# One next-key projection chunk spread over the attention groups of a turn, and the lead part's scores spaced by width

## The chip, the cores and the metric

The kernel runs on one core of a Trainium2 chip. The metric is the device time of one launch in microseconds. Three runs of the kernel before took 3239.09, 3241.71 and 3245.02 us; the median, 3241.71 us, is the time to compare with. TensorE (PE) multiplies, VectorE (DVE) and ScalarE (ACT) empty PSUM and do the elementwise work, GpSimd (POOL) splits weights, SyncE (SP) issues the weight loads.

## The reference, cut to what matters

Two blocks run one after the other on 1024 tokens of width 1024. The two parts that the change touches are attentions with 16 heads of width 64:

```
# block 1: forgetting attention ("fox"), causal, 128-token blocks
logits = q k^T * scale + F[t] - F[s];  probs = softmax(masked logits);  o = probs v
y_f = o * silu(g)
# block 2, second mixer ("nb"): 2-D neighbourhood attention with a relative bias,
# 8 rows x 16 columns of keys around each query, plus 256 context tokens
s = q k^T * scale + bias;  p = softmax([s, s_ctx]);  o = p [v, v_ctx];  y = (o * silu(g)) w_out
```

q, k, v and g are projections of the same input (`u @ w_in`). Everything else (the recurrent branch, the windowed mixer, output projections, norms) is outside the change.

## The kernel before, in words

Every float32 product is done as three fast products of high and low parts: w_hi u_hi, w_hi u_lo, w_lo u_hi. A weight unit is 128 output columns (one pair of heads). SP loads units in a fixed order, POOL splits each into w_hi and w_lo (L210, L212) into one of two slots, as soon as PE signals that the unit two places earlier is used up. A projection chunk is 8 tiles x 3 parts = 24 matmuls (FULL) of up to 512 columns into one PSUM bank; its last matmul signals.

Both attentions are instances of one class, Flow, each with 8 turns (one for each pair of heads). A planner (`plan`) writes one list of steps for a turn, and PE, ACT and DVE each walk it in this order, doing their share and waiting on semaphores:

- F n: PE does the next n matmuls of the projection stream (L1304). For fox the stream in a turn is V0 V1 G0 G1 of this turn, then Q0 Q1 K0 K1 of the next (192 matmuls); nb has V0 V1 V2, G0 G1, Q0 Q1, K0 K1 K2 (240; V2 and K2 are the 256 context columns). Chunks of a turn alternate between two PSUM banks, and a chunk's first matmul waits until the chunk two places earlier has been taken out.
- E: a finished chunk is taken out. For a key or query chunk ACT casts the high part (L1578, L1581, L2423, L2426) and DVE subtracts the low part (L1602, L1606, L2470, L2474). Key and query chunks finished before the turn's last score are held until it has been issued.
- S: a piece of scores on PE (L1334), then DVE's masked reduction of it (L1455). The next S on PE waits for that reduction. The first S of a turn also waits for the last key chunk's low part.
- X: ACT's exponential (L1384). T: transposes on PE (L1350; L1345 for v, L1355 for the row sums), cast on ACT (L1393), low part on DVE (L1466). V: probs times v on PE (L1368).
- I, M, O, N: inverse row sums (L1484, L1486), the half swap of the output (L1407), its sum (L1494) and its product with the inverse sums (L1479).
- W, Y, D: silu on ACT (L1411); y times silu on DVE (L1504), then ACT's cast of y (L1416); D is DVE's low part of y (L1509) and ACT's two stores (L1426).
- L, B: ACT's load of the next turn's mask rows, and DVE's preparation of them in two parts (L1614 for fox, two instructions a part in L2450 and L2453 for nb).

A turn has three parts. The lead runs 24 matmuls for each V chunk, with the four score pieces of segment 0 at places 6 to 49 of the stream. The groups (20 in fox, 26 in nb) are one T each, with S, V and fill spread so that after the last group the stream stands at `main`: the end of the Q chunks. The tail runs what is left: K0 and K1 (and K2) stand beside the last events, W, Y, D and B. The last of the eight turns has no Q or K.

In fox, before the change, the steps from the last V on are: V, L, F4 N F4 I F4 M F4 O F4 N, W, Y, F4, E(K0), D, B, F24, E(K1), B, and the next turn begins F6 S F8 S. In nb they are V, L, F4 M F4 O F4 N, W, Y, F12, E(K0), D, B, F24, E(K1), B, F24, E(K2), then F6 S F14 S.

Of the kernel before, what the change touches and what calls it, by code (L numbers as in the profile page):

```python
# [15 lines left out]
P = 128  # L16
# [39 lines left out]
def build_program(nc, a):  # L56
# [3 lines left out]
    def sb(name, shape, dt=F32, at=None):  # L60
        return (at or ctx).enter_context(nc.sbuf_tensor(name, shape, dt))
# [4 lines left out]
    with ctx:  # L66
# [234 lines left out]
        scores = sb("scores", [P, 8, P], at=ph2)  # L301
# [690 lines left out]
        class Flow:  # L992
# [110 lines left out]
            def plan(self, before, turns, final, tables, last_fill, side_by_side=False):  # L1103
# [5 lines left out]
                FULL = 3 * KT  # L1109
# [3 lines left out]
                def chunks_of(units, scores_before, side_by_side=False):  # L1113
                    new = []
                    parts = [(unit, i) for unit in units for i in range(len(unit[3]))]
                    if side_by_side:
                        parts.sort(key=lambda part: part[1] >= 2)
                    for (kind, it, unit, spans), i in parts:
                        c0, n = spans[i]
                        last, seq = i == len(spans) - 1, len(self.chunks)  # L1120
                        beside = side_by_side and seq < 4
                        b = (self.p_bank, self.p_bank + 1, self.o_bank, self.o_bank + 1)[seq] if beside \
                            else self.p_bank + seq % 2
                        count[final[kind]] += 1
                        count["chunk"] += not last
                        ch = {"kind": kind, "it": it, "unit": unit, "c0": c0, "n": n, "first": i == 0,
                              "last": last, "seq": seq, "scored": scores_before, "bank": b, "beside": beside,
                              "waits": self.user.get(b),
                              "done": (w_used, unit + 1) if last else (self.chunk, count["chunk"]),
                              "out": ({"act": self.act_out, "dve": self.dve_out}[final[kind]], count[final[kind]])}  # L1130
                        self.user[b] = ch["out"]
                        self.chunks.append(ch)
                        new.append(ch)
                    return new

                def group(kind, it, **more):
                    g = {"kind": kind, "n": count["G"], "it": it, **more}
                    count["G"] += 1
                    if kind != "N":
                        count["high"] += 1  # L1140
                        g["high"] = count["high"]
                    return g
# [11 lines left out]
                for it, units in enumerate(turns):  # L1154
                    fill = chunks_of(units, count["S"] + n_scores)
                    steps, held = [], []
                    at = {"fill": 0, "S": 0}

                    scores, base_u = [], count["U"]
# [11 lines left out]
                    def fill_to(n):  # L1171
                        n = min(n, FULL * len(fill))
                        while at["fill"] < n:
                            part = min(n - at["fill"], FULL - at["fill"] % FULL)
                            steps.append(("F", part))
                            at["fill"] += part
                            if at["fill"] % FULL == 0:
                                ch = fill[at["fill"] // FULL - 1]
                                if ch["kind"] in "QK" and at["S"] < n_scores:
                                    held.append(ch)  # L1180
                                else:
                                    steps.append(("E", ch))

                    def score(s):
                        s["l_free"] = l_turned[s["seg"] % 2]
                        steps.append(("S", s))
                        at["S"] += 1
                        if at["S"] == n_scores:
                            steps.extend(("E", ch) for ch in held)

                    def exponentials(n):
                        while due and n:
                            steps.append(("X", *due.pop(0)))
                            n -= 1
# [1 line left out]
                    due, final_turn = [], it == len(turns) - 1  # L1196
                    values = [ch for ch in fill if ch["kind"] == "V"]
                    lead = FULL * len(values)
                    places = [(6 + (lead - 14) * i // len(scores[0]), "S", s) for i, s in enumerate(scores[0])]
                    places += [(FULL * (i + 1) + 9, "T", ch) for i, ch in enumerate(values)]  # L1200
                    for pos, what, x in sorted(places, key=lambda place: place[0]):
                        fill_to(pos)
# [7 lines left out]
                    exponentials(4)  # L1210
                    groups = [self.seg_groups(seg) for seg in range(len(self.segments))]
                    n_groups = sum(len(g) for g in groups)
                    start, main = at["fill"], FULL * sum(ch["kind"] in "VGQ" for ch in fill)
                    if final_turn:
                        n_groups = last_fill
                    todo, waiting, done = [], None, 0
# [1 line left out]
                    def event():  # L1218
                        if todo:
                            what, *rest = todo.pop(0)  # L1220
                            steps.append(("T", group("N", it, seg=rest[0], seg_n=rest[1])) if what == "N" else
                                         (what, *rest))

                    for seg, rows in enumerate(groups):
                        count["seg"] += 1
                        pending = list(scores[seg + 1]) if seg + 1 < len(scores) else []
                        for i, (items, adds) in enumerate(rows):
                            g = group("P", it, seg=seg, seg_n=count["seg"], items=items, adds=adds, starts=i == 0,
                                      ends=i == len(rows) - 1, exped=base_u + self.first_unit(seg + 1))
                            steps.append(("T", g))  # L1230
                            l_turned[seg % 2] = g["n"] + 1
                            exponentials(1)
                            share = -(-len(pending) // (len(rows) - i))
                            for s in pending[:share]:
                                score(s)
                                due += [(s, hd) for hd in range(2) if s["end"]]
                            del pending[:share]
                            done += 1
                            goal = start + (main - start) * min(done, n_groups) // n_groups
                            fill_to((at["fill"] + goal) // 2)  # L1240
                            if i == 0:
                                todo.append(("I", seg, g["exped"]))
                            if waiting:
                                steps.append(("V", waiting))
                                if waiting["ends"]:
                                    s0 = (waiting["seg"], waiting["seg_n"])
                                    todo[-1:-1] = [("M", it, *s0), ("O", it, *s0), ("N", *s0)]
                                    if self.early and final_turn and seg == len(groups) - 1:
                                        todo.append(("W", it))
                                        for part, cols in enumerate(self.early):  # L1250
                                            todo += [("D", it, self.early[part - 1])] if part else []
                                            todo.append(("Y", it, cols))
                                event()
                            waiting = g
                            fill_to(goal)
                            if i == len(rows) - 1:
                                exponentials(4)
# [1443 lines left out]
```

## Time and profile before

| | |
|---|---|
| median of three runs | 3241.71 us |
| profiled execution, first to last instruction (span) | 3236.3 us |
| PE busy | 3109.7 us, 96% |
| DVE busy | 1999.7 us, 62% |
| ACT busy | 1299.9 us, 40% |
| POOL busy | 759.8 us, 23% |
| mean granted TensorE clock | 0.988 |

The span is one execution, 5.4 us shorter than the median run. Busy time of PE counts overlapping matmuls once, and their ends are modelled, so starts are what to read. "Idle before" stands in brackets behind a row, with what ended it. Fox's turns run from 601.7 to 1209.2 us, nb's from 2346.2 to 3095.4 us.

### The profile page before, as it was taken

The numbers are of one execution on the slowest core, as the hardware profiler recorded it, in microseconds if no ns is written. First come the engines' busy times: TensorE is split into PE (matmuls) and PEld (weight loads), VectorE is DVE, ScalarE is ACT, GpSimd is POOL, SyncE is SP. The second block draws the span as 40 slices with busy tenths as digits, with TensorE's granted clock in tenths as the row PEclk, the third lists the DMA queues.
The fourth block names the chain that finished last, engine by engine and source line by source line (L and its number), as shares of the span: only waits on it lengthen the run. The fifth ranks groups of instructions, "written<-read, shape, count | busy, mean of one in ns | idle before, by whom it ended". The sixth has DMA issues, their size and how long they took to land.

```text
span 3236.3 us, 47842 instructions
## 1 busy us (share of the span) xinstructions
PE 3109.7 (96%) x18134; PEld 2578.9 (80%) x18134; DVE 1999.7 (62%) x3834; ACT 1299.9 (40%) x2340; POOL 759.8 (23%) x324
## 2 busy tenths in 40 slices
PE   9999999999999989999899999999899999999987
PEld 6888888777777767877799889888677778777765
DVE  5676677555565657975755555556755555655555
ACT  5534443444444440022444444440344444454412
POOL 3223332322222213543211121113112112111221
PEclk9999999999999999999999999999999999999999
DMA  3111111111111137521200010153201111100141
GB/s 118 46 40 46 46 59 46 60 59 53 53 53 53 64 146 298 220 79 52 91 30 30 31 43 30 46 203 130 78 21 51 45 51 45 51 32 33 67 161 76
DMA packets 64828, 237.79 MB, mean 73 GB/s; under 512 B 7008, under 2 KB 10080, under 8 KB 63600
## 3 DMA queue, kind: packets, MB, share of 16 engines
q1 hardware_dynamic: 31680, 115.91, 9.9%
q10 hardware_dynamic: 32944, 119.10, 9.7%
q8 instruction: 135, 2.21, 0.3%
q14 instruction: 69, 0.57, 0.0%
HBM read 185.11 MB, written 49.87 MB: 73 GB/s over the span
## 4 chain that ended last, share of the span: by engine, by line
PE 79%; DVE 9%; ACT 5%; issue 2%; DVEq 2%; DMA 1%; ACTq 1%; SPq 0%
PE ps L1304 21%; PE ps L189 13%; PE ps L360 9%; PE ps L2223 7%; PE ps L1368 5%; PE ps L1334 4%; PE ps L1350 4%; PE ps L891 3%; PE ps L482 3%; PE ps L868 2%; PE ps L133 2%; DVE fox_l L1455 1%; PE ps L852 1%; DVE wa_l L941 1%; PE ps L853 1%
## 5 line engine op out<-in xcount | busy, mean ns | idle before, releaser
L210 POOL TENSOR_TENSOR w_hi<-raw,small 128x1024 fp32r<-128x1024 f32 x160 | 334.9, 2093 | 2393.7 <-PE ps L1304 1099.3
L212 POOL TENSOR_TENSOR w_lo<-raw,w_hi 128x1024 fp32r<-128x1024 f32 x160 | 424.8, 2655 | 22.8
L1304 PE MATMUL ps<-nb_u_hi,w_hi 128*128 128x512 f32 (+1 forms) x640 | 249.2, 389 | 6.1 <-DVE nb_q_lo L2470 4.2
L1304 PE MATMUL ps<-nb_u_hi,w_lo 128*128 128x512 f32 (+1 forms) x640 | 246.6, 385 | 0.0
L1304 PE MATMUL ps<-nb_u_lo,w_hi 128*128 128x512 f32 (+1 forms) x640 | 245.7, 384 | 0.0
L1466 DVE TENSOR_TENSOR nb_pt_lo<-ps,nb_pt_hi 128x512 fp32r<-128x512 f32 x208 | 143.9, 692 | 144.2 <-ACT nb_pt_hi L1393 143.9
L360 PE MATMUL ps<-u_hi,w_hi 128*128 128x512 f32 x528 | 212.8, 403 | 5.9 <-ACT silu_h L539 2.6
L1304 PE MATMUL ps<-u_hi,w_lo 128*128 128x512 f32 x512 | 208.9, 408 | 0.0
L360 PE MATMUL ps<-u_hi,w_lo 128*128 128x512 f32 x528 | 208.6, 395 | 0.0
L360 PE MATMUL ps<-u_lo,w_hi 128*128 128x512 f32 x528 | 208.4, 395 | 0.0
L1304 PE MATMUL ps<-u_hi,w_hi 128*128 128x512 f32 x512 | 208.3, 407 | 0.0
L1304 PE MATMUL ps<-u_lo,w_hi 128*128 128x512 f32 x512 | 207.5, 405 | 0.0
L1393 ACT CAST nb_pt_hi<-ps 128x512 fp32r<-128x512 f32 x208 | 122.1, 587 | 193.4 <-PE ps L1350 190.7
L1466 DVE TENSOR_TENSOR fox_pt_lo<-ps,fox_pt_hi 128x512 fp32r<-128x512 f32 (+1 forms) x160 | 102.0, 638 | 129.3 <-ACT fox_pt_hi L1393 128.8
L2223 PE MATMUL ps<-wa_u_hi,w_hi 128*128 128x512 f32 (+1 forms) x480 | 173.1, 361 | 4.3 <-DVE wa_u_lo L2156 1.9
L891 PE MATMUL ps<-wa_v,wa_pt 128*128 128x64 f32 x1344 | 176.5, 266 | 0.0
L2223 PE MATMUL ps<-wa_u_lo,w_hi 128*128 128x512 f32 (+1 forms) x480 | 171.1, 356 | 0.0
L2223 PE MATMUL ps<-wa_u_hi,w_lo 128*128 128x512 f32 (+1 forms) x480 | 171.0, 356 | 0.0
L902 ACT ACTIVATE wa_l<-wa_l,wa_nm 128x641 f32<-128x641 f32 (+2 forms) x160 | 119.3, 746 | 124.8 <-DVE wa_nm L941 123.6
L891 PEld LDWEIGHTS ps<-wa_v,wa_pt 128*128 128x128 f32 x1344 | 168.9, 192 | 0.0
L1393 ACT CAST fox_pt_hi<-ps 128x512 fp32r<-128x512 f32 (+1 forms) x160 | 87.0, 544 | 144.8 <-PE ps L1350 144.3
L1304 PEld LDWEIGHTS ps<-nb_u_hi,w_hi 128*128 128x128 f32 x640 | 121.6, 190 | 29.3 <-issue 11.6
(357 smaller groups left out, 8027.8 us busy)
## 6 DMA issues: line engine op xcount, KB each, us to landing
raw<-in_w_stream SPq DMA_DIRECT2D x160, 512.0 KB, 3.3
h_sb<-in_w_ada ACTq DMA_DIRECT2D x16, 1024.0 KB, 5.0
nf_b<-nf_rows ACTq DMA_DIRECT2D x16, 512.0 KB, 4.4
nb_bias<-in_rel_bias ACTq DMA_DIRECT2D x16, 448.0 KB, 3.8
y_parts<-wa_y_hi ACTq DMA_DIRECT2D x8, 640.0 KB, 3.0
y_parts<-wa_y_lo ACTq DMA_DIRECT2D x8, 640.0 KB, 4.2
la_out_yh<-y_parts SPq DMA_DIRECT2D x8, 640.0 KB, 10.0
la_out_yl<-y_parts SPq DMA_DIRECT2D x8, 640.0 KB, 11.1
```

The costliest lines, as they stand in the source:

```text
L189: mm = pe.matmul(out, w(slot, tiles[i]), u[:, first + i, cols], start=start and i == 0 and p == 0, stop=stop and i == len(tiles) - 1 and p ...
L210: pool.tensor_tensor(w_hi[:, s, :], raw[:, s, :], zero, ALU.add)
L212: pool.tensor_tensor(w_lo[:, s, :], raw[:, s, :], w_hi[:, s, :].bitcast(F32), ALU.subtract).then_inc(w_ready, 1)
L360: mm = pe.matmul(ps[:, b:b + CH], w(slot, k), u[:, k, ch["c"] * CH:(ch["c"] + 1) * CH], start=k == 0 and p == 0, stop=k == KT - 1 and p == 2)
L891: mm = pe.matmul(ps[:, o0:o0 + HD], self.pt[0:n, self.v_place[g] % 3, (c - c0) * P:(c - c0 + 1) * P], vals[0:n, vb, cols], start=c == 0, s ...
L1304: mm = pe.matmul(ps[:, b:b + ch["n"]], w(slot, k), u[:, k, ch["c0"]:ch["c0"] + ch["n"]], start=k == 0 and p == 0, stop=k == KT - 1 and p == 2)
L1334: mm = pe.matmul(ps[:, o:o + n], q[r, qc], k[r, key:key + n], start=p == 0, stop=p == 2)
L1350: mm = pe.transpose(out[:, j * P:(j + 1) * P], self.l_of(g["seg"], qi, hd)[:, l0:l0 + P], ident)
L1368: mm = pe.matmul(ps[:, o + o0:o + o0 + n], self.v[:, vb, kv if self.shared else hd, :], pt[:, g["high"] % 2, p0:p0 + n], start=g["starts"] ...
L1393: nc.scalar.copy(self.pt_hi[:, g["high"] % 2, 0:w], ps[:, t:t + w]).then_inc(self.high, 1)
L1466: dve.tensor_tensor(self.pt_lo[:, i, 0:w], ps[:, t:t + w], self.pt_hi[:, i, 0:w].bitcast(F32), ALU.subtract).then_inc(self.freed, 1)
L2223: mm = pe.matmul(ps[:, b * CH + t:b * CH + t + n], w(i % 2, k), u[:, k, t:t + n], start=k == 0 and p == 0, stop=k == KT - 1 and p == 2)
```

## The change

Two edits in `plan`; a third line changes no order, since no piece of segment 0 is ever in the list of a later segment.

```diff
-                    places = [(6 + (lead - 14) * i // len(scores[0]), "S", s) for i, s in enumerate(scores[0])]
+                    ahead = scores[0]
+                    sizes = [sum(n for _, _, n in s["blk"]["pieces"][s["piece"]]["runs"]) + 3 * P // 2 for s in ahead]
+                    places = [(6 + (lead - 14) * sum(sizes[:i]) // sum(sizes), "S", s) for i, s in enumerate(ahead)]
...
-                    start, main = at["fill"], FULL * sum(ch["kind"] in "VGQ" for ch in fill)
+                    first_k = [ch for ch in fill if ch["kind"] == "K"][:1]
+                    start, main = at["fill"], FULL * (sum(ch["kind"] in "VGQ" for ch in fill) + len(first_k))
...
-                        pending = list(scores[seg + 1]) if seg + 1 < len(scores) else []
+                        pending = [s for s in scores[seg + 1] if s not in ahead] if seg + 1 < len(scores) else []
```

Score places in the lead (in matmuls of the stream): fox 6, 14, 23, 31 become 6, 17, 22, 33 (widths 512, 128, 512, 256); nb 6, 20, 35, 49 become 6, 23, 35, 52 (widths 512, 256, 512, 256). In seven of eight turns of each flow `main` grows by 24, from 144 to 168 in fox and from 168 to 192 in nb: chunk K0 is now done between the groups, and the tail has one 512-column key chunk less. The tail's steps are now, in fox: V, L, F4 N F4 I F4 M F4 O F4 N, W, Y, F4, E(K1), D, B, B, and the next turn begins F6 S F11 S. In nb: V, L, F4 M F4 O F4 N, W, Y, F12, E(K1), D, B, F24, E(K2), B, then F6 S F17 S. No instruction is added or removed on any engine.

## Rows read from the trace of the kernel before

**Rows 1.** The page, busy time of each engine (us, share, instructions).
```profile
PE 3109.7 (96%) x18134; PEld 2578.9 (80%) x18134; DVE 1999.7 (62%) x3834; ACT 1299.9 (40%) x2340; POOL 759.8 (23%) x324
```

**Rows 2.** Stretch, length, busy PE PEld DVE ACT POOL, clock, DMA: fox, nb groups.
```profile
850.60:897.90 47.30, 46.03 (x293) 36.76 (x292) 29.05 (x88) 23.84 (x55) 6.56 (x4) 1.00 0.07 23
...
2653.40:2714.20 60.80, 58.80 (x408) 47.17 (x406) 38.89 (x94) 31.62 (x61) 7.51 (x4) 1.00 0.05 18
```

**Rows 3.** Waits of PE, fox turn 832.0:909.4 (total us, times, longest).
```profile
PE ps L1334 <- DVE fox_nm L1455: 0.9, 3, 0.4
PE ps L1350 <- DVE fox_pt_lo L1466: 0.6, 1, 0.6
```

**Rows 4.** Waits of PE, nb turn 2632.7:2728.2.
```profile
PE ps L1350 <- ACT nb_l L1384: 1.4, 2, 0.8
PE ps L1334 <- DVE nb_nm L1455: 0.5, 1, 0.5
```

**Rows 5.** Timeline of PE, end of a fox turn (start, duration, ..., idle before).
```profile
903.98 0.39 PE L1304 MATMUL ps<-u_hi,w_hi 128*128 128x512 f32 x1
...
909.47 0.39 PE L1304 MATMUL ps<-u_hi,w_hi 128*128 128x512 f32 x1
...
911.13 0.49 PE L1334 MATMUL ps<-fox_k_hi,fox_q_hi 64*128 64x512 f32 x2
...
914.43 0.33 PE L1334 MATMUL ps<-fox_k_hi,fox_q_hi 64*128 64x128 f32 x2 [0.29 <-DVE fox_nm L1455]
```

**Rows 6.** Timeline of ACT, the same stretch.
```profile
905.10 1.05 ACT L1416 CAST fox_y_hi<-fox_y 128x1024 fp32r<-128x1024 f32 x1 [3.27 <-DVE fox_y L1504]
906.05 0.58 ACT L1581 CAST fox_k_hi<-ps 128x512 fp32r<-128x512 f32 x1
```

**Rows 7.** Timeline of DVE, the same stretch.
```profile
903.84 1.23 DVE L1504 TENSOR_TENSOR fox_y<-fox_y,fox_silu 128x1024 f32<-128x1024 f32 x1
906.66 0.69 DVE L1606 TENSOR_TENSOR fox_k_lo<-ps,fox_k_hi 128x512 fp32r<-128x512 f32 x1 [1.60 <-ACT fox_k_hi L1581]
907.27 1.22 DVE L1509 TENSOR_TENSOR fox_y<-fox_y,fox_y_hi 128x1024 f32<-128x1024 f32 x1
908.40 1.22 DVE L1614 TENSOR_TENSOR nf_tri<-nf_b,consts 128x1024 f32<-128x1024 f32 x1
...
910.90 1.86 DVE L1614 TENSOR_TENSOR nf_tri<-nf_b,consts 128x1024 f32<-128x1024 f32 x1
912.94 0.75 DVE L1455 CUSTOM_DVE_ANT_0 fox_l<-ps,nf_b,fox_top 128x512 f32<-128x512 f32 x1 [0.18 <-issue]
```

**Rows 8.** Timeline of POOL, the same stretch.
```profile
909.78 1.89 POOL L210 TENSOR_TENSOR w_hi<-raw,small 128x1024 fp32r<-128x1024 f32 x1 [7.53 <-PE ps L1304]
911.82 3.19 POOL L212 TENSOR_TENSOR w_lo<-raw,w_hi 128x1024 fp32r<-128x1024 f32 x1
```

**Rows 9.** Timeline, fox's third segment: a transpose group of PE, a low part of DVE.
```profile
889.11 0.60 PE L1350 MATMUL ps<-consts,fox_l 128*128 128x128 f32 x4
...
889.67 0.69 DVE L1602 SCALAR_TENSOR_TENSOR fox_q_lo<-ps,fox_q_hi 128x512 fp32r<-128x512 f32 x1
```

**Rows 10.** Timeline of DVE, end of an nb turn.
```profile
2722.61 2.09 DVE L2450 TENSOR_TENSOR nb_bias<-nb_bias,consts 128x896 f32<-128x896 f32 x2
...
2728.85 0.42 DVE L2474 TENSOR_TENSOR nb_k_lo<-ps,nb_k_hi 128x256 fp32r<-128x256 f32 x1 [0.34 <-ACT nb_k_hi L2426]
```

**Rows 11.** Timeline of PE, the first score of the nb turn that follows.
```profile
2729.71 0.50 PE L1334 MATMUL ps<-nb_k_hi,nb_q_hi 64*128 64x512 f32 x2
```

**Rows 12.** Timeline of POOL beside four back-to-back DVE subtractions (L1850).
```profile
1404.46 2.48 POOL L210 TENSOR_TENSOR w_hi<-raw,small 128x1024 fp32r<-128x1024 f32 x1 [5.68 <-PE ps L189]
```

**Rows 13.** Timeline of DVE, the same stretch.
```profile
1403.97 8.54 DVE L1850 TENSOR_TENSOR r_lo<-h_sb,r_hi 128x1024 fp32r<-128x1024 f32 x4
```

**Rows 14.** A long wait of PE elsewhere in the kernel, and the stretch around it.
```profile
1259.77 0.79 PE L189 MATMUL ps<-y_hi,w_hi 128*128 128x512 f32 x1 [3.34 <-DMA y_lo<-y_parts]
```

**Rows 15.** Busy time by stretch around that wait (columns as in rows 2).
```profile
1259.00:1264.00 5.00, 4.23 (x12) 3.38 (x13) 0.37 (x1) 0.00 (x0) 1.97 (x1) 0.66 1.03 409
```

## The prediction

> **What bounds the kernel now.** I read the page first: PE is busy 96% of the span, the next engine 62% [rows 1]. So PE's order sets the time, and an edit of the order can only change how long PE waits. Then the busy time by stretch: in a fox turn the groups take 47.30 us, of which PE is idle 1.3; in an nb turn 60.80 with 2.0 idle [rows 2]. The waits of PE give the reasons. A fox turn has 0.9 us for the reduction of scores (three waits, one of them the 0.29 in the lead) and 0.6 for a low part [rows 3]; an nb turn 1.4 us for exponentials and 0.5 for a reduction [rows 4]. The tails show no wait at all. All turns are alike, so one stands for seven. What the groups can give back at most is 7 x 1.3 + 7 x 1.9 = 22 us. What the tail hides must be read from ACT, DVE and POOL there.
>
> **Unit of the sum.** A full key chunk takes PE 909.47 - 903.98 = 5.49 us, 0.229 a matmul [rows 5]. PE's work stays the same. The change takes 5.49 us out of each tail and puts it between the groups, so anything in the tail that was less than 5.49 us early becomes late.
>
> **Fox, end of the turn.** DVE multiplies y by silu from 903.84 to 905.07 [rows 7]. ACT casts y from 905.10 and only then takes out the key chunk (906.05 to 906.63) [rows 6]; DVE's low part ends at 907.35 [rows 7]. Before, that chunk is K0, and K1 with its 5.49 us still follows. Now it is K1, and the next turn's first score needs it. PE would like that score at 911.13 - 5.49 = 905.64 and gets it about 0.1 after 907.35: a wait of 1.8 us where there was hardly one. The whole row y, cast, key cast, key low part keeps its place, because it hangs on PE's steps after the last V, which are the same.
>
> The second score waits for DVE's reduction of the first. Between them DVE still has D (1.22) and the two mask preparations (1.22 each, the 1.86 being a delayed one) [rows 7], and none of these now stands beside K1. Free of delay they end at 910.9, the reduction (begun 0.18 later, 1.5 for two heads) at 912.5. PE, with F11 in place of F8, would like the second score at 907.45 + 0.9 + 11 x 0.229 + 0.2 = 911.1. That is a wait of 1.4, where 0.4 was (0.29 shown [rows 5] and the least gap that is not shown): 1.0 more.
>
> Now POOL. It starts a split 0.31 us after the first matmul behind the last key chunk (909.78 against 909.47) [rows 5, 8]. DVE's second mask instruction, begun at 910.90, took 1.86 and ended 1.1 after POOL's 1.89 us instruction: it waited for POOL's end and then ran its 1.22. POOL's next one took 3.19 [rows 8], and had to wait in turn. So a subtraction or addition with both inputs in SBUF and POOL's split exclude each other. The Trainium skill, "SBUF — State Buffer", section "SBUF: two separate sides", says this as a rule: whichever starts first keeps the shared port for its whole instruction and the other fully blocks; the trace agrees, 1.86 against 1.22. With K1 done 5.49 earlier the split begins at 904.29, beside y times silu, waits for its end at 905.07, and its second instruction begins near 907.0, 0.3 us before D (907.27). That one takes about 2.4 (3.19 less its wait of 0.8), so D begins at 909.35, not 907.27, and the second score waits 2.1 more. I take this: 1.0 + 2.1 + 0.1 for the drains = 3.2 for the second score. The other end is 1.0.
>
> **Fox, groups.** Half-groups go from F2 to F3. Two waits on reductions and some gaps too short to be shown lose one matmul, 0.23 each: about -0.7. The pt_lo wait of 0.55 in the third segment is different: Q1 now ends there too. Q0 is held until the last score and its low part ends at 889.67 + 0.69 = 890.36 [rows 9]. K0 uses the same bank, and its first matmul comes right behind Q1, where PE now has transposes (889.11) [rows 9]: it waits 1.3 us. This swallows the 0.55. Net of the groups: -0.7 - 0.6 + 1.3, with the small gaps -0.2 at most; bounds -1.3 (all waits gone, none new) and +0.3. Fox a turn: 1.8 + 3.2 - 0.2 = 4.8; seven turns 34 us.
>
> **nb, end of the turn.** One more chunk (K2, 24 short matmuls) stands behind K1, so K1's cast is no problem. The first score would like to start at 2729.71 - 5.49 = 2724.2 [rows 11]. DVE's two mask additions run 2722.61 to 2724.70 and K2's low part (0.42) is queued behind them [rows 10]: the score starts at 2725.2, a wait of 1.0. That is the lower end. POOL's split now arrives at 2723.1, in the first of the two. In the other place where POOL arrived during back-to-back SBUF subtractions, it went in after the first: four of 1.22 took 8.54 us [rows 13], and POOL's took 2.48 [rows 12]. Then the second addition is 1.9 late, and the wait is 2.9, with 0.2 behind it: 3.1. I take 2.7, nearer to the row. **nb, groups:** the extra matmul stands in each stretch in which a wait ended, and the two waits for exponentials (0.7 each) lose two matmuls or the cast of a gate chunk ahead of them: -0.4 each, the reduction -0.2, small gaps -0.4: -1.4 (bounds 0 and -1.9 shown, -2.5 with the small gaps). nb a turn: 2.7 - 1.4 = 1.3; seven turns 9 us.
>
> **The spacing by width** moves fox's second score by 3 matmuls, which is counted above; alone it would save the 0.3 of [rows 5]. In nb's leads and in turn 0 nothing waits, so it costs nothing; its cover is the 2 us and more between each reduction's end and the next score. DMAs: the same loads and stores from the same queue; y's stores go out 2 us later in fox, and the next turn needs y's buffer only in its second segment. The mask rows are asked for at the last V and needed about 10 us later.
>
> **Clock.** After a wait of 3.34 us [rows 14] PE ran at a mean of 0.66 over 5 us [rows 15], 1.2 GHz for 3.4 us, against 2.4 before: 5 x 0.34 = 1.7 us lost. The fox junction now has a wait of about 3.3 us, two and a half us after one of 1.8. I count the fall in half of the seven turns: 6 us. Bounds: none, and all 14 junctions, 24.
>
> **Sum.** 34 + 9 + 6 = 49 us on the profiled execution: span 3236.3 to 3285. That execution is 5.4 below the median; the same 49 on 3241.7 gives **3291 us**, 1.5% slower.
>
> **Rivals.**
> (a) POOL and DVE miss each other: the order of arrivals shifts by 0.3 us and D goes first. For: 0.3 us is little. Against: the rows repeat to 0.02 us, and a POOL instruction then only waits and blocks the mask additions. Fox 1.8 + 1.0 - 0.2 = 2.6, nb 1.0 - 1.4 = -0.4: 18 - 3, so 3257.
> (b) The clock falls at every junction. For: nb's wait is near 3 us. Against: nb's wait is shorter than the 3.34 of that row. 43 + 24: 3309.
> (c) Faster: the tail's chain y, cast, key cast runs early enough, and only the groups' gain is left. It decides at one point: whether DVE starts y times silu at least 1.8 us sooner than 903.84 when counted from the last V. For: the other split, of the V unit, started at the turn's last V before and now comes earlier, so DVE's steps of the tail have POOL beside them less. Against: y hangs on PE's last pair of transposes, which keeps its place. Fox -1.3, nb -1.4 to -1.9: -20, so 3222.
> (d) No measurable change: the new waits are as long as the old ones, both flows near 0; 3242. It needs (a) and half of (c).
>
> **From cases to numbers.** My forecast 0.62, (a) 0.17, (b) 0.09, (c) 0.06, (d) 0.06. The forecast's own range, by the bounds of nb (1.0 to 3.1), of fox's groups (-1.3 to +0.3) and the clock (0 to 12), is 3270 to 3302. For 8 in 10 I add (a) and most of (b): **3254 to 3308**. About 0.2%, 6.5 us, is what can be told from no change here: faster 0.06, the same 0.06, slower 0.88.
>
> **What would show it.** In the profile after: at each fox junction a wait of PE for k_lo of about 2 us, then one for the reduction (nm) of about 3.3; D in fox taking about 3.3 us instead of 1.22 and a POOL instruction of 2.6 just before; a wait of 1.3 at a projection matmul in fox's third segment for q_lo; nb's first score waiting 1 to 3 us for the low part of K2; nb's waits for exponentials down from 1.4 to about 0.6 a turn. I am wrong if the first score of a fox turn starts within 0.5 us of when PE reaches it, or if fox turns (77 us before, the stretch of [rows 3]) are shorter than 78.

## The result: 1.9% slower, and the profile after

The changed kernel takes 3303.82 us (median of 5 runs, 3298.78 to 3313.21) beside 3244.45 us before (5 runs); the ratio is 1.0189 [1.0173, 1.0204]. The forecast was 3291 us, a change of +49; measured are +59 between the medians and +67 between the two profiled spans. Its profiled execution took 3305.42 us. The measured time lies just above the forecast's own range (3270 to 3302) and inside the wider one (3254 to 3308). In the kernel after, the lines of Flow stand 3 lower: L1337 is L1334 of before. "First score" of a turn is its first S, "second score" the next one.

| | before | after |
|---|---|---|
| span of the profiled execution | 3236.3 us | 3303.6 us |
| mean granted TensorE clock | 0.988 | 0.978 |
| first score to first score, fox turns | 77.0 us | 81.8 to 84.4 us (the first one 78.4) |
| first score to first score, nb turns | 95.5 us | 96.8 to 99.8 us |

The busy line of the page answers to [rows 1]. PE is busy 26 us more for the same 18134 instructions. The work is the same and the mean granted clock is lower, so more of it ran at the lower clock.

```profile
PE 3136.0 (95%) x18134; PEld 2599.5 (79%) x18134; DVE 2017.2 (61%) x3834; ACT 1304.3 (39%) x2340; POOL 765.7 (23%) x324
```

The waits of PE over the whole program (total us, times, longest): the first three did not exist at this size before. Each stands at the seven junctions between turns (the second has the short waits of [rows 3] in it too). The fourth, once in each of seven fox turns, is the new wait for the shared PSUM bank.

```profile
PE ps L1337 <- DVE nb_k_lo L2477: 18.5, 7, 2.6
PE ps L1337 <- DVE fox_nm L1458: 18.2, 16, 3.3
PE ps L1337 <- DVE fox_k_lo L1609: 13.8, 7, 2.0
PE ps L1307 <- DVE fox_q_lo L1605: 8.5, 7, 1.2
```

The end of a fox turn, PE first. It answers to [rows 5]: the first score waits 1.97 us; its first pair of matmuls takes 0.70 us where it took 0.49, because the clock falls to half just then. The second starts 7.00 us after the first, where it was 3.30.

```profile
931.08 0.70 PE L1337 MATMUL ps<-fox_k_hi,fox_q_hi 64*128 64x512 f32 x2 [1.97 <-DVE fox_k_lo L1609]
...
938.08 0.33 PE L1337 MATMUL ps<-fox_k_hi,fox_q_hi 64*128 64x128 f32 x2 [1.78 <-DVE fox_nm L1458]
```

DVE in the same place, against [rows 7]: the chain y times silu, low part of the key, D, two mask preparations, reduction is the same, but D takes 3.12 us and not 1.22.

```profile
927.42 1.22 DVE L1507 TENSOR_TENSOR fox_y<-fox_y,fox_silu 128x1024 f32<-128x1024 f32 x1
930.24 0.69 DVE L1609 TENSOR_TENSOR fox_k_lo<-ps,fox_k_hi 128x512 fp32r<-128x512 f32 x1 [1.60 <-ACT fox_k_hi L1584]
930.85 3.12 DVE L1512 TENSOR_TENSOR fox_y<-fox_y,fox_y_hi 128x1024 f32<-128x1024 f32 x1
933.90 2.51 DVE L1617 TENSOR_TENSOR nf_tri<-nf_b,consts 128x1024 f32<-128x1024 f32 x2
936.59 0.75 DVE L1458 CUSTOM_DVE_ANT_0 fox_l<-ps,nf_b,fox_top 128x512 f32<-128x512 f32 x1 [0.18 <-issue]
```

POOL shows why, against [rows 8]. Its first instruction, issued beside y times silu, ends at 930.40; the second holds from 930.54 to 932.89, and D ends 1.08 us after that (933.97), about the time that it takes alone. D took 3.12 to 3.15 us in all seven junctions.

```profile
927.88 2.52 POOL L210 TENSOR_TENSOR w_hi<-raw,small 128x1024 fp32r<-128x1024 f32 x1 [12.58 <-PE ps L1307]
930.54 2.35 POOL L212 TENSOR_TENSOR w_lo<-raw,w_hi 128x1024 fp32r<-128x1024 f32 x1
```

The end of an nb turn, against [rows 10, 11]: DVE's two mask additions take 3.79 us where they took 2.09, because POOL, which arrives during the first one, gets in ahead of the second. K2's low part is queued behind them, and the first score waits 2.65 us.

```profile
2782.22 3.79 DVE L2453 TENSOR_TENSOR nb_bias<-nb_bias,consts 128x896 f32<-128x896 f32 x2
2786.08 0.42 DVE L2477 TENSOR_TENSOR nb_k_lo<-ps,nb_k_hi 128x256 fp32r<-128x256 f32 x1
```

```profile
2782.76 2.29 POOL L210 TENSOR_TENSOR w_hi<-raw,small 128x1024 fp32r<-128x1024 f32 x1 [16.18 <-PE ps L1307]
```

```profile
2786.65 0.51 PE L1337 MATMUL ps<-nb_k_hi,nb_q_hi 64*128 64x512 f32 x2 [2.65 <-DVE nb_k_lo L2477]
```

The groups with K0 in them and then the tail, by stretch (columns as in [rows 2]), for the fox turn that ends at the junction above.

```profile
868.65:921.50 52.85, 51.42 (x317) 41.30 (x316) 29.72 (x89) 24.70 (x56) 10.77 (x5) 1.00 0.08 31
921.50:927.57 6.07, 6.07 (x30) 4.97 (x30) 2.82 (x8) 3.53 (x5) 0.00 (x0) 1.00 0.49 175
```

Before, the tail behind the groups of [rows 2] was this:

```profile
897.90:909.45 11.55, 11.55 (x54) 9.46 (x54) 8.79 (x11) 5.06 (x7) 4.21 (x2) 1.00 0.44 142
```

Together that is 52.85 + 6.07 = 58.9 us, and before 47.30 + 11.55 = 58.9. The groups have the 24 matmuls more (x317 where it was x293); the chunk has moved, and nothing was saved.

In nb the waits of one turn (window from before one first score to after the next, so that the first line counts two) went down as forecast, against [rows 4]: 1.4 to 0.6 and 0.5 to 0.3.

```profile
PE ps L1337 <- DVE nb_k_lo L2477: 5.3, 2, 2.6
PE ps L1353 <- ACT nb_l L1387: 0.6, 2, 0.4
PE ps L1337 <- DVE nb_nm L1458: 0.3, 1, 0.3
```

The clock: two stretches behind such waits, in nb and in fox, columns as before.

```profile
2491.00:2498.00 7.00, 6.45 (x18) 4.72 (x19) 4.97 (x7) 0.00 (x0) 2.13 (x1) 0.51 0.24 78
931.10:934.60 3.50, 3.50 (x11) 2.43 (x12) 3.50 (x2) 0.00 (x0) 1.79 (x1) 0.52 0.12 41
```

The granted clock fell to 1.2 GHz (0.5) for 3.4 to 6.8 us at all seven fox junctions and at five of seven in nb. Before, it fell at none of the 14.

### The profile page after: what moved, and what is told of

It reads as the page before. It is cut to its first block, busy times and chain, and to the rows that moved or that the text cites. A ratio compares the mean times of both kernels' runs of the same rounds, so it can differ in the third digit from the quotient of the medians.

```text
span 3303.6 us, 47842 instructions
## 1 busy us (share of the span) xinstructions
PE 3136.0 (95%) x18134; PEld 2599.5 (79%) x18134; DVE 2017.2 (61%) x3834; ACT 1304.3 (39%) x2340; POOL 765.7 (23%) x324
## 4 chain that ended last, share of the span: by engine, by line
PE 79%; DVE 10%; ACT 4%; issue 2%; DVEq 2%; DMA 1%; ACTq 1%; SPq 0%
PE ps L1307 20%; PE ps L189 13%; PE ps L360 9%; PE ps L2226 7%; PE ps L1371 5%; PE ps L1337 5%; PE ps L1353 4%; PE ps L891 3%; PE ps L482 3%; PE ps L868 2%; PE ps L133 2%; PE ps L852 1%; DVE fox_l L1458 1%; PE ps L853 1%; DVE wa_l L941 1%
## 5 line engine op out<-in xcount | busy, mean ns | idle before, releaser
L210 POOL TENSOR_TENSOR w_hi<-raw,small 128x1024 fp32r<-128x1024 f32 x160 | 342.2, 2139 | 2453.5 <-PE ps L1307 1153.7
```

Of the source, the lines that this page charges most:

```text
L210: pool.tensor_tensor(w_hi[:, s, :], raw[:, s, :], zero, ALU.add)
```

## The experiments

The twelve kernels are each made from the changed one. Where only one part of an edit is shown, the rest is said, and `...` marks lines left out. "Turn" below is the time from one turn's first score to the next one's. In the kernels that spread fox's chunk the first turn is shorter than the others, because its own second score doesn't wait. Ratios are to the runs of the kernel before that were taken beside each experiment, with medians of 3243 to 3244 us.

**1. Spacing alone.**

```diff
-                    first_k = [ch for ch in fill if ch["kind"] == "K"][:1]
+                    first_k = []
```

> Only the lead's scores are spaced by width; the key chunk stays in the tail. My theory (the whole loss is the chunk taken from the tail): fox's second score has F11 in place of F8 before it, so its wait of 0.29 us goes in seven turns, nothing changes in nb: 2 to 3 us less than before, within 0.1%. Rival (the spacing itself costs, because later scores of the lead and their exponentials move towards the groups): 5 to 15 us more than before, and a longer wait of nb's first transposes for exponentials.

3238.16 us, ratio 0.9985 [0.9976, 0.9993]. The fox turn is 76.6 us and not 77.0, as the second score no longer waits: 2.4 us over the seven turns (538.8 to 536.4). nb's turn stays 95.5. The medians differ by 4.8 us; the rest of that shows in no turn. This half of the change, which has no term of its own in the sum, is a small gain by itself.

**2. Chunk alone, scores at the old places.**

```diff
-                    places = [(6 + (lead - 14) * sum(sizes[:i]) // sum(sizes), "S", s) for i, s in enumerate(ahead)]
+                    places = [(6 + (lead - 14) * i // len(scores[0]), "S", s) for i, s in enumerate(ahead)]
```

> Only the key chunk is spread; the lead's scores stand as before. My theory: fox's second score starts when DVE is done with the first, whatever PE does before it, so this takes the time of the changed kernel within 3 us (about 3303), with the wait before the second score longer by the three matmuls that stand behind it instead of before it. Rival (the spacing carries a part of the loss): 3295 or less.

3320.66 us, 1.0234 [1.0217, 1.0252], 17 us above the changed kernel, which neither the theory nor its rival expected. The second score is again 7.03 us behind the first, since DVE decides that, but PE reaches it three matmuls earlier and waits 4.04 us where the longest wait was 3.3:

```profile
944.61 0.47 PE L1337 MATMUL ps<-fox_k_hi,fox_q_hi 64*128 64x128 f32 x2 [4.04 <-DVE fox_nm L1458]
```

The three matmuls (0.69 us) now stand behind the wait. And at all seven fox junctions the clock falls during this wait and stays low for 5 to 6 us behind it, over work that PE is late with:

```profile
944.60:951.40 6.80, 6.79 (x23) 4.80 (x24) 1.01 (x5) 1.73 (x4) 0.00 (x0) 0.56 0.05 21
```

The turn is up to 85.3 us, 3.4 more than the 81.9 of a fox turn of the changed kernel in which the fall costs nothing. Over the seven fox turns it is 14.5 us (589.5 beside 575.0), while nb's stay the same (685.5 and 685.7). So inside the changed kernel the spacing saves some 15 us, much more than alone.

**3 and 4. Fox alone, nb alone.** The line of experiment 1, with `[:1] if self.name == "fox" else []`, then with `"nb"`.

> The key chunk is spread in fox alone; the spacing is in both. My theory: 34 us of waits at seven junctions and about 9 of lower clock behind them: 3244 + 43 = 3287, nb as before (95.5 us a turn). Rival (the two flows share the loss evenly): 3273.

> The key chunk is spread in nb alone; the spacing is in both. My theory: each turn loses 2.65 us before the first score and gains 1.3 in the groups, 9 us in all, and the clock costs about as much again: 3244 + 18 = 3262. If the clock did not fall behind these waits, 3253. Rival (even share): 3273.

3289.69 us, 1.0141 [1.0126, 1.0156], and 3260.58 us, 1.0057 [1.0041, 1.0072]. Above the before of their session (3242.96 us) that is 46.7 and 17.6 us, as expected. The sum, 64, has the spacing's gain of 4.8 us in it twice; with it counted once, 69, the intervals of the three medians just meet that of the whole change (56 to 66). The turns are the sharper test: with fox alone its seven turns take 577.9 us (575.0 in the changed kernel) and nb's 668.8 (668.6 before); with nb alone nb's take 686.1 (685.7) and fox's 536.5 (536.4 in experiment 1). The two flows don't touch each other, and nb costs more than the 9 us forecast for it.

**5. Key chunk before y.** In fox the step Y (y times silu and its cast) stands behind E(K1).

```diff
-                    steps += [("W", it), ("Y", it, self.whole)]
+                    steps.append(("W", it))
...
                     fill_to(FULL * (at["fill"] // FULL + 1))
+                    if self.name == "fox":
+                        steps.append(("Y", it, self.whole))
```

> The changed kernel, with fox's y (silu product and cast) put behind the last key chunk's evacuation, so that the first score no longer waits for it. My theory (two links in a row: take one away and DVE's chain of y, its low part and the masks holds the second score): the wait before the first score falls from 2.0 to about 0.4 us, the second score starts 0.5 us later than before counted from the turn's first matmul (its wait about 5.5), and the time is 3303 to 3315. Rival (the cast behind y is the cause by itself): 7 x 1.6 = 11 us and some clock less than the changed kernel, 3290 or below.

3312.42 us, 1.0212 [1.0194, 1.0231]. The first wait is gone (0.12 us, as before the change); the second is 5.39. The time is as the theory had it, and the rival is out: the vector work ahead of the reduction is the limit, and letting the first score through earlier only moves the wait.

```profile
941.96 0.48 PE L1341 MATMUL ps<-fox_k_hi,fox_q_hi 64*128 64x128 f32 x2 [5.39 <-DVE fox_nm L1462]
```

**6. A short D.** Turns 0 to 6 subtract only 8 of 1024 columns in D; the rest of y's low part is left out, in both flows.

```diff
+                        if it < PAIRS - 1:
+                            y = y[:, 0:8]
+                            dve.tensor_tensor(y, y, self.y_hi[:, 0:8].bitcast(F32),
+                                              ALU.subtract).then_inc(self.lo_done, 1)
+                            continue
```

> The changed kernel, with y's low part made over 8 columns only in turns 0 to 6 of both flows (the rest of the low part is left out), which takes 1.2 us of DVE's work out of the junction. My theory (POOL's second split instruction holds whichever DVE instruction with two SBUF inputs comes first): in fox the tiny subtraction, or the mask addition behind it, is blocked until the same moment, so the second score starts only 1.2 us earlier. Rival (the subtraction itself is slow there, no exclusion): it starts 3.1 us earlier. In nb the mask additions end before POOL arrives, and the 2.6 us before the first score go. Time by my theory about 3267, by the rival 3254.

One run, 3274.07 us (expected 3267). In fox the second score comes 5.95 us after the first, 1.05 sooner: D's own work is saved, POOL's hold is not. The rows show DVE first, then POOL: the subtraction over 8 columns takes 2.07 us and ends at 928.62, and POOL's instruction ends at 928.61. A fox turn in which the clock doesn't fall is 80.8 us.

```profile
926.55 2.07 DVE L1514 TENSOR_TENSOR fox_y<-fox_y,fox_y_hi 128x8 f32<-128x8 f32 x1
```

```profile
926.24 2.37 POOL L212 TENSOR_TENSOR w_lo<-raw,w_hi 128x1024 fp32r<-128x1024 f32 x1
```

In nb, where no POOL instruction runs at that time, the same subtraction takes 0.16 us. So it isn't slow by itself:

```profile
2764.11 0.16 DVE L1514 TENSOR_TENSOR nb_y<-nb_y,nb_y_hi 128x8 f32<-128x8 f32 x1
```

In nb the first score no longer waits, but the second now does (1.3 us for the reduction), and the turn is 95.6, as before the change. These are fox's two scores:

```profile
926.78 0.49 PE L1337 MATMUL ps<-fox_k_hi,fox_q_hi 64*128 64x512 f32 x2 [1.97 <-DVE fox_k_lo L1614]
...
932.73 0.33 PE L1337 MATMUL ps<-fox_k_hi,fox_q_hi 64*128 64x128 f32 x2 [0.72 <-DVE fox_nm L1458]
```

**7. PE kept busy in the waits.** Matmuls of a constant, into banks that are free then, ahead of the late scores. The rest of the edit marks these scores as `busy`: in turns 1 to 7 the first one, and in fox the second too.

```diff
+                        if s["busy"] and s["head"]:
+                            pe.wait_ge(self.shifted, s["n"] - 1)
+                            keep_busy(pe, self.s_bank, 16 if self.name == "fox" else 22)
+                        elif s["busy"]:
+                            pe.wait_ge(self.freed, s["g"])
+                            keep_busy(pe, self.t_bank, 26)
```

> The changed kernel, with small matmuls of constants on PE while it waits for the first score (fox 16, nb 22) and for fox's second (26), into banks that are free then. They end before the waits do. My theory (clock falls behind the waits cost 17 to 19 us): scores start at the same distance from the turn's first matmul, the granted clock stays 1.00 through the leads, all fox leads take 22.9 us and all nb leads 23.3, and the time is 3285. Rival (the falls lie in waits anyway and cost nothing): 3303.

3329.11 us, 1.0262 [1.0245, 1.0279]: 44 us above the 3285 expected, and inconclusive. The clock stayed at 1.00 at the junctions, but the filler was twice as long as meant and outlasted the waits (the second score came 9.42 us after the first). Each constant matmul is two instructions of about 0.11 us.

**8. The same with half the counts** (8, 11 and 13).

> The changed kernel with constant matmuls ahead of the waits of turns 1 to 7, half as many as in the first run of this kind: 8 (1.8 us) before fox's first score, 13 (2.9 us) before its second, 11 (2.4 us) before nb's first. They end before the data does, so the ends of the waits stay. Theory (the clock's falls cost 19 us: 8 in fox's leads, 2 in its last groups, 9 in nb's leads): granted clock 1.00 in every junction, fox leads 22.9 and nb leads 23.3 in all turns, 3283 to 3288. Rival (my 6 us were right, and the other 13 are waits of another kind): 3296 to 3300, with leads still above 23.5 at full clock.

3290.77 us, 1.0149 [1.0133, 1.0164]. Now the ends of the waits stay where they were (second score 7.02 us after the first), and the clock stays at 1.00 with them:

```profile
925.97 1.95 PE L120 MATMUL ps<-ones_mean 128*128 128x128 f32 x16
928.11 0.50 PE L1346 MATMUL ps<-fox_k_hi,fox_q_hi 64*128 64x512 f32 x2 [0.19 <-DVE fox_k_lo L1618]
...
931.63 3.06 PE L120 MATMUL ps<-ones_mean 128*128 128x128 f32 x26
935.13 0.33 PE L1346 MATMUL ps<-fox_k_hi,fox_q_hi 64*128 64x128 f32 x2 [0.43 <-DVE fox_nm L1467]
```

```profile
608.00:1220.00 612.00, 593.34 (x3519) 476.14 (x3518) 333.88 (x917) 272.68 (x552) 132.82 (x60) 1.00 0.17 58
```

This is the cleanest reading of the change: every fox turn after the first (78.4) is now 81.8 or 81.9 us and every nb turn 96.9. Beside the changed kernel the seven fox turns are 5.4 us shorter (575.0 to 569.6), the seven of nb 7.2 (685.7 to 678.5), and of the last turns, which end the two flows, fox's is 3.7 and nb's 1.4 us shorter: 17.7 us between the two profiled executions. The medians differ by 13.0. So the lower clock costs 13 to 18 us; the 17 to 19 expected is at or above the top of that, and the 6 of the prediction far too low. The time is 3 us above the 3283 to 3288 expected.

**9. Masks early.** L stands at the last segment's first group. Fox's two B stand ahead of the last O, nb's in the last segment's fifth and sixth group.

> The changed kernel, with the next turn's mask rows loaded at the last segment's first group, and their preparation on DVE put into fox's tail ahead of the last output sum and into nb's last segment. My theory (DVE's queue at the junction sets the starts): fox's second score starts 2.0 to 2.4 us earlier, nb's first score waits 0.2 instead of 2.6, a good part of the clock falls go with them, and nb's last segment gains up to 2 us of waits for low parts: 3262 to 3278. Rival (the key chunk's evacuation alone sets both): no change, 3303.

3268.75 us, 1.0077 [1.0060, 1.0094], inside the 3262 to 3278 expected. The best fox turn is 79.6. There the first score waits 2.4 us, 0.45 more than in the changed kernel, because the mask preparations now stand ahead of y; and the second comes 4.32 us after it, because they no longer stand ahead of its reduction. At two of the seven junctions the first score waits 4.2 us. There POOL's first instruction starts 0.13 us (once 0.33) ahead of y times silu, which then takes 2.84 us (2.64), and D 1.22; at the other five y times silu starts 0.01 or 0.02 us ahead, takes 1.23, and D takes 3.13 to 3.15.

```profile
838.76 2.84 DVE L1512 TENSOR_TENSOR fox_y<-fox_y,fox_silu 128x1024 f32<-128x1024 f32 x1
```

```profile
838.63 1.89 POOL L210 TENSOR_TENSOR w_hi<-raw,small 128x1024 fp32r<-128x1024 f32 x1 [12.59 <-PE ps L1312]
```

So with arrivals this close the order of the two engines changes from turn to turn within one execution, and each order delays a different score. The nb turn is 95.8; the first wait is nearly gone (0.2), but with the mask additions in the groups PE waits once or twice for a low part (pt_lo), 0.8 and 0.6 us.

**10. All late vector work out of the way, both flows.** L as in 9. In the tail B stands behind the last O (nb: its second part behind y times silu). In fox E(K1) comes next, Y behind the next turn's second score, D behind the third; in nb D behind the second. `moved` is True here.

```diff
+                            k = ahead.index(x)
+                            if it and self.name == "nb" and k == 1:
+                                steps.append(("D", it - 1, self.whole))
+                            if True and it and self.name == "fox" and k in (1, 2):
+                                steps.append(("YD"[k - 1], it - 1, self.whole))
...
-                    steps.append(("L", it + 1, count["S"]))
+                    if moved:
+                        todo[-1:-1] = [("B", it + 1, p) for p in range(1 if self.name == "nb" else 2)]
```

> The changed kernel with its chunk spread in both flows, and the work that became late taken out of the way of the first two scores. Mask rows are loaded at the last segment's first group. Fox: both mask preparations behind the last sum O and ahead of the last product N; the last key chunk is taken out next; y times silu, its cast behind the next turn's second score, the low part D behind the third. nb: one part of the masks behind O, the other behind y times silu, D behind the next turn's second score. Theory (the 7 us a fox turn and 2.6 an nb turn are order and the shared port alone, nothing is due to the chunk's move itself): fox's first score waits 0 to 0.4 us, the second 0 to 0.5, leads 18.0 to 18.6 as before, groups and tail 58.3 to 58.7; nb's first score waits under 0.3, period 1.3 below before's 95.5. Sum: fox 0 to +4, nb -9: 3235 to 3240 beside a before of 3244.5. Rival (moving a key chunk between the groups costs PE whatever the order of the others, or the moved vector work collides elsewhere): some 2 us a fox turn stay, 3250 or more.

3280.5 us, 1.0112 [1.0095, 1.0128]: my number was 40 us off, and the trace says where. No score at a junction waits any more, as forecast. But ACT walks the same list. It stood at y's cast and then at the stores, which wait for DVE's D. Behind these were exponentials (with 1.28 us for a table load) and the copy of V0 that PE's transposes need:

```profile
936.12 0.33 ACTq L1446 DMA_DIRECT2D y_parts<-fox_y_hi  x1
936.48 0.45 ACTq L1446 DMA_DIRECT2D y_parts<-fox_y  x1
...
939.89 0.57 ACT L1603 COPY fox_vt<-ps 128x512 f32<-128x512 f32 x1
```

```profile
940.60 0.63 PE L1365 MATMUL ps<-consts,fox_vt 128*128 128x128 f32 x4 [3.85 <-ACT fox_vt L1603]
```

The fox turn is 82.1 = 76.6 + 3.85 for this wait + 1.7 for the clock behind it (the mean is 0.66 over the five us that follow). The first turn, in which no y of an earlier turn is late, is 76.6 us, that of experiment 1. In that one turn the moved chunk costs fox nothing and gains nothing; a kernel that shows it for the others was not tried.

**11. nb alone, reordered.** As 10 in nb; fox keeps its chunk in the tail and its old order.

> The chunk spread in nb alone, with nb's masks and low part reordered as in the run before; fox keeps its chunk in the tail and its old order, with the scores spaced by width in both. Theory: spacing gives 3 to 6 us as in the run of the spacing alone, nb's groups give back 1.3 us a turn and its first score no longer waits, 7 to 9 us: 3229 to 3235 beside a before of 3244.5, faster than both kernels. Rival: the masks ahead of the last product delay nb's y and with it the next score, or D in the lead delays the third score, 1 us a turn or more: 3239 or more.

3241.78 us, 0.9996 [0.9987, 1.0005]: not the 3229 to 3235 of the theory, but in the rival's range, for a reason that neither named. It is the same fault at ACT: PE waits 1.3 us in seven turns for the copy of V0. Most turns are 95.7 us, and the first, which has no D of an earlier turn, is 94.2.

**12. The stores later.** As 11, with D cut in two: DVE's subtraction stays, ACT's stores go behind the cast of the first V transposes.

```diff
-                                steps.append(("D", it - 1, self.whole))
+                                steps.append(("Dd", it - 1, self.whole))
...
                             steps.append(("T", group("VT", it, chunk=x)))
+                            if it and self.name == "nb" and x is values[0]:
+                                steps.append(("Da", it - 1, self.whole))
```

> The run with nb alone spread and reordered, with one change: ACT's two stores of y (they wait for DVE's low part D, now behind the second score) stand behind the cast of the first V transposes instead of ahead of V0's copy. Theory (the 1.3 us wait of the V transposes in 7 turns is ACT held by these stores, and nothing else is left of the change's cost in nb): that wait gone, an nb period of 94.2 us where before has 95.5, and 9 us less than that run: 3230 to 3235 beside a before of 3244.4, faster than both kernels. Rival (the stores then hold the exponentials of the first segment, or the next wait takes the place): the period stays near 95.5, 3239 or more.

3233.30 us, 0.9962 [0.9949, 0.9976]: as expected, and faster than both kernels, by 10.7 us than before. Six nb turns take 94.3 us and one 95.0, where before has 95.5; that is 7.8 us, and 2.3 more come from the spacing in fox (536.5 beside 538.8). All waits of PE in one of the six, first score to first score, against [rows 4]:

```profile
PE ps L1370 <- ACT nb_l L1404: 0.6, 2, 0.4
PE ps L1354 <- DVE nb_nm L1475: 0.3, 1, 0.3
```

Fox with ACT's part of Y and D also put later was not tried.

## Why the prediction was right, and where it was off

- **The bound.** PE's order sets the time and the change adds only waits: right. With the clock held (experiment 8) its cost is 30.8 us in the seven fox turns (569.6 - 538.8), 3 in the last turn for its second score, and 9.9 in nb (678.5 - 668.6): 44 us, where the sum had 34 + 9 = 43.
- **Fox, first score:** predicted 1.8, measured 1.97.
- **Fox, second score:** predicted 3.2 more, to about 3.3. It is 3.0 more: the longest wait is 3.3 us, where 0.29 was. Where the clock had fallen already it reads 1.78, because the matmuls ahead of it fill the gap at half pace. It ends 7.00 us after the first score either way. The meeting with POOL is as argued: a POOL instruction of 2.35 (predicted 2.4 from about 907.0) and a D of 3.12 us (about 3.3). That D is late by POOL's hold, not by its length, is what experiment 6 shows: 8 columns took 2.07 us beside POOL and 0.16 without it.
- **Fox, groups:** -0.2 predicted, 0 measured (58.9 us for groups and tail in both kernels); the new bank wait is 1.2 (1.3).
- **nb:** first score 2.65 (2.7), groups -1.3 (-1.4). The choice between a wait of 1.0 and 3.1 fell on the right side, because POOL did get in after the first of two back-to-back additions, as in [rows 12, 13].
- **Clock: the term that was mis-sized.** I put falls at half of the fox junctions and none in nb, 3.5 in all and 6 us. The trace shows them at 12 of 14 junctions, and experiment 8 prices them at 13 to 18 us. The argument that nb's wait is shorter than the 3.34 us of [rows 14] was no protection: it fell at waits of 2.65 us and, in fox, of 1.97. And rival (b), all 14 at 1.7, would have been too dear: at three of the seven fox junctions the one fall lies behind the first score, and its loss is inside the wait for the second, where it costs nothing.
- **The spacing:** right that alone it is worth 0.3 a turn, wrong as a full account. I had put fox's three matmuls into the sum of the second wait, but not what they save at the clock: the changed kernel without the spacing is 17 us slower (experiment 2). Of this 7 x 0.69 = 4.8 us are the matmuls themselves.
- **The range.** Its own bounds, added up, give 3265 to 3303 and not 3270 to 3302. The measured 3303.8 is just above it: the clock was bounded at 12 us in that range, and cost 13 to 18.

The clean 44 and the clock's 13 to 18 make 57 to 62, beside 59 between the medians. Of the 67 us between the two profiled spans 62 lie in the two flows. The other 5.7 lie outside them, 4.2 between the end of fox and the start of nb and 1.9 behind nb, which the change doesn't touch. The stretch between fox and nb took 1140 to 1148 us in eight of the kernels here (before, after and six of the experiments), in no order that follows the edits; I give this part no cause. Rivals (a), (c) and (d) are out: D did meet POOL at all seven fox junctions, and y times silu came no sooner behind the last V. The 0.3 us that rival (a) called little held in every one of these turns; experiment 9 shows the order changing where the two starts lie 0.02 us apart.

## What to carry to other kernels

When matmuls are moved out of a tail, list what the other engines did beside them. PE's work in a turn didn't change by the move; what changed was that the vector, scalar and GpSimd work beside it lost 5.49 us of cover. Move that work too, and look at every engine that walks the list. Experiments 10 and 11 mended DVE's order, but ACT stood at a store: PE waited 27 us for it in fox and 9 in nb in experiment 10, with the lower clock behind the waits in fox, and 9 us in nb in experiment 11. And count a new wait of about 2 us or more in a dense stretch of matmuls (1.97 was the shortest at which the clock fell at a junction here) at its length plus half of the stretch behind it that runs at the lower clock, but only if PE is the late engine there.

## What the runs showed of the hardware

- Waits of 1.97 and 2.65 us were enough for the granted clock to fall to 1.2 GHz for 3.4 us, and sometimes for 6.8. The same wait did and did not bring a fall in different turns (2.65 us in nb: five of seven; 2.4 us in experiment 9: one of five). The seven waits of 1.3 us in nb in experiment 6 brought none. Filling the gaps with constant matmuls kept it at 1.00 at all 14 junctions, and saved 13 us with work of no other use (experiment 8).
- A float32 matmul of constants is two instructions of about 0.11 us: 8 of them were 16 instructions, 1.95 us.
- DVE's subtraction D took 1.22 us alone and 3.12 beside POOL's split. The Trainium skill, "SBUF — State Buffer", section "SBUF: two separate sides", has the two engines share one port, which whichever starts first holds for its whole instruction. The trace agrees, most plainly with the 8 columns that took 2.07 us (0.16 without POOL, experiment 6) and with the two junctions of experiment 9 where POOL started first.
